# RWKV scan of a hybrid encoder step: head pairs on the column halves for the sample state, one y product for both chunks of a tile

## The reference, cut to what matters

```
def step(S, inp):                       # S: 64 x 64 per head, 8 heads
    r_t, w_t, k_t, v_t, kk_t, a_t = inp
    sa = einsum('bhij,bhj->bhi', S, -kk_t)
    S = S * w_t + sa (x) (kk_t * a_t) + v_t (x) k_t
    return S, einsum('bhij,bhj->bhi', S, r_t)      # y
S_fin, ys = lax.scan(step, S0, ...)
```

## Time and profile before

| what | value |
|---|---|
| median of 3 runs | 4723.28 us (4710.8 to 4728.6) |
| span of the profiled execution | 4722.2 us, 74875 instructions |
| median less the span | 1.1 us |
| PE busy | 4342.7 us, 92% of the span |
| DVE, ACT, POOL busy | 48%, 35%, 17% |
| mean granted TensorE clock | 0.971 of full speed |
| the eight sample state blocks (L1089 to L1091) | 5.72 us each |
| L1106, the y products of the chunks | x512 passes |

### The profile page before, as it was taken

The page is one execution under the profiler, slowest core; times in us unless marked ns, Lnnn a source line. Parts: engine busy times, 40 slices in busy tenths (PEclk is TensorE's granted clock), DMA queues, the critical chain, the costliest instruction groups (busy, mean ns, idle before and its releaser), DMA issues. The chain is left out here.

```text
span 4722.2 us, 74875 instructions
## 1 busy us (share of the span) xinstructions
PE 4342.7 (92%) x29488; PEld 3013.1 (64%) x29488; DVE 2275.1 (48%) x4684; ACT 1644.4 (35%) x3886; POOL 813.5 (17%) x980
## 2 busy tenths in 40 slices
PE   7999997989889989999979999979898899899999
PEld 3656665667666667777436666646676566677774
DVE  2555664345524463434425556643455344535344
ACT  4333333345533442212043333333555233421220
POOL 0011010000010015444300110000000100145443
PEclk8999998999999999999989999989999999999999
DMA  5110111110021112232241200120100211223222
GB/s 194 23 34 10 26 29 60 41 34 14 13 87 52 58 58 98 91 105 76 85 191 23 34 12 28 25 85 15 35 14 12 87 56 54 75 86 113 87 71 85
DMA packets 150654, 280.77 MB, mean 59 GB/s; under 512 B 51545, under 2 KB 77401, under 8 KB 145058
## 3 DMA queue, kind: packets, MB, share of 16 engines
q1 hardware_dynamic: 150306, 275.99, 18.3%
HBM read 230.96 MB, written 42.62 MB: 58 GB/s over the span
## 5 line engine op out<-in xcount | busy, mean ns | idle before, releaser
L1054 PE MATMUL banks<-hT,w_piece 128*128 128x384 f32 x1536 | 549.0, 499 | 8.4 <-ACT raw L1158 8.2
L1054 PEld LDWEIGHTS banks<-hT,w_piece 128*128 128x128 f32 x1536 | 281.4, 194 | 178.5 <-issue 15.1
L2232 PE MATMUL banks<-hT,w_piece 128*128 128x384 f32 x1056 | 354.1, 489 | 1.4 <-ACT sb_gate_raw L2342 1.4
L2232 PEld LDWEIGHTS banks<-hT,w_piece 128*128 128x128 f32 x1056 | 196.1, 190 | 141.4 <-issue 16.6
L1998 DVE SCALAR_TENSOR_TENSOR keysT<-banks,gains,rstd 64x128 f32<-64x128 f32 (+1 forms) x272 | 112.0, 412 | 248.1 <-ACT rstd L1912 245.5
L2688 DVE TENSOR_TENSOR gate_quarters<-gate_kept,banks 128x288 f32<-128x288 f32 x144 | 65.4, 454 | 299.0 <-PE banks L2551 294.0
L2639 ACT ACTIVATE gate_kept<-banks 128x288 f32<-128x288 f32 x144 | 59.1, 411 | 431.5 <-PE banks L2551 431.5
L2688 DVE TENSOR_TENSOR branch_quarters<-branch_kept,banks 128x288 f32<-128x288 f32 x144 | 65.4, 454 | 265.3 <-PE banks L2551 265.2
L2404 DVE TENSOR_TENSOR_SCAN left<-pass,zero 128x384 f32<-128x384 f32 (+7 forms) x144 | 189.8, 1318 | 5.0
L2401 DVE TENSOR_TENSOR pass<-pass,constants 128x128 f32<-128x128 f32 x128 | 41.5, 324 | 309.9 <-ACT take L2353 307.4
L1015 POOL TENSOR_TENSOR state_decayed<-state,decay_of_chunk 128x128 f32<-128x128 f32 x120 | 85.9, 716 | 578.7 <-DVE state L1287 578.7
(11 more groups left out here) (425 smaller groups left out, 9803.7 us busy)
## 6 DMA issues: line engine op xcount, KB each, us to landing
w_piece<-in_w_cols SPq DMA_DIRECT2D x66, 512.0 KB, 4.4
w_ada<-in_w_ada SPq DMA_DIRECT2D x24, 1024.0 KB, 10.5
w_gate_ahead<-in_w_cols SPq DMA_DIRECT2D x48, 512.0 KB, 4.3
w_branch<-in_w_br SPq DMA_DIRECT2D x96, 256.0 KB, 2.9
w_gate<-in_w_cols SPq DMA_DIRECT2D x48, 512.0 KB, 4.3
y_branch<-y_gated SPq DMA_DIRECT2D x12, 1152.0 KB, 8.4
sb_cached_keysT<-in_sbkT SPq DMA_DIRECT2D x8, 1024.0 KB, 7.6
sb_cached_values<-in_sbv SPq DMA_DIRECT2D x8, 1024.0 KB, 5.3
```

The lines of the kernel that those rows point to most:

```text
L1054: last = mm(dst, w[0 if kind in ("k", "v") else 1][:, k, :], hT[:, k, c], start=(k == 0), stop=(k == KD - 1))
L2232: last = mm(ps[:, bank[n], 0:TG], w_of[wn][:, k, :], hT[:, k, TG * g:TG * g + TG], start=(k == 0), stop=(k == KD - 1))
```

## The change: order of the sample products, and the y products

Three things are done. The sample products are issued head by head within each step rather than step by step within each head, in both places. The y products of even chunks are dropped, and those of odd chunks cover both chunks of the tile: 128 moving columns as two runs of 64 (`TM[:, i, 2:4, hc]`), two products per tile instead of four. For that both chunks' U write the same bank, `y_bank(i)`, in its columns 0 to 127 and 128 to 255; the second U has `start=False`. ACT and DVE follow the new places, and `y_ready` counts tiles instead of chunks.

```
+        def y_bank(i):
+            return 4 - 2 * (i % 2)
...
-            for hh in range(2):
-                hc = slice(64 * hh, 64 * hh + 64)
+            for hh, hc in enumerate(HALVES):
                 mm(ps[:, 4 + hh, :], R.WS[hc, :], S0[hc, :], start=True, stop=True)
+            for hh, hc in enumerate(HALVES):
                 last = mm(ps[:, 6 + hh, :], rows_of(RW[hc], i, 3), S0[hc, :], start=True, stop=True)
...
-            for hh in range(2):
-                hc = slice(64 * hh, 64 * hh + 64)
+            for hh, hc in enumerate(HALVES):
                 mm(ps[hc, 4, :], TM[:, i, 0, hc], wide[hh]..., start=True, stop=False, ...)
+            for hh, hc in enumerate(HALVES):
                 mm(ps[hc, 4, :], TM[:, i, 1, hc], wide[2 + hh]..., start=False, stop=False, ...)
+            for hh, hc in enumerate(HALVES):
                 last = mm(ps[hc, 4, :], ident[hc, hc], S0[hc, :], start=False, stop=True, ...)
...
-                ub = 4 + c - 2 * (i % 2)
-                if i >= 2:
+                yb = y_bank(i)
+                if c == 0 and i >= 2:
                     pe.wait_ge(y_copied, i - 1)
-                mm(ps[:, ub, 0:P], rows_of(RW, i, 4 - 2 * c), ST[:, :], start=True, stop=True).then_inc(u_ready, 1)
+                mm(ps[:, yb, P * c:P * c + P], rows_of(RW, i, 4 - 2 * c), ST[:, :], start=(c == 0), stop=True, ...).then_inc(u_ready, 1)
...
-                for hh in range(2):
-                    hc = slice(64 * hh, 64 * hh + 64)
-                    last = mm(ps[:, ub, hc], SI[:, i, hh, :], TM[:, i, 2 + c, hc], start=False, stop=True, ...)
-                last.then_inc(y_ready, 1)
+                if c == 1:
+                    both = ps[:, yb, 0:2 * P].rearrange("p (c n) -> p c n", c=2)
+                    for hh, hc in enumerate(HALVES):
+                        last = mm(both[:, :, hc], SI[:, i, hh, :], TM[:, i, 2:4, hc], start=False, stop=True, ...)
+                    last.then_inc(y_ready, 1)
```

More of the change, by code:

```diff
@@ L1096, in _ @@
                 pe.wait_ge(s_scaled, n + 2)
-                ub = 4 + c - 2 * (i % 2)
-                if i >= 2:
+                yb = y_bank(i)
+                if c == 0 and i >= 2:
                     pe.wait_ge(y_copied, i - 1)
-                mm(ps[:, ub, 0:P], rows_of(RW, i, 4 - 2 * c), ST[:, :], start=True, stop=True).then_inc(u_ready, 1)
+                mm(ps[:, yb, P * c:P * c + P], rows_of(RW, i, 4 - 2 * c), ST[:, :], start=(c == 0), stop=True, skip_group_check=True).then_inc(u_ready, 1)
                 fill(mid)
@@ L1103, in _ @@
                 mm(ps[:, 6, 0:P], TM[:, i, c, :], TM[:, i, 2 + c, :], start=True, stop=True).then_inc(s_ready, 1)
-                for hh in range(2):
-                    hc = slice(64 * hh, 64 * hh + 64)
-                    last = mm(ps[:, ub, hc], SI[:, i, hh, :], TM[:, i, 2 + c, hc], start=False, stop=True, skip_group_check=True)
-                last.then_inc(y_ready, 1)
+                if c == 1:
+                    both = ps[:, yb, 0:2 * P].rearrange("p (c n) -> p c n", c=2)
+                    for hh, hc in enumerate(HALVES):
+                        last = mm(both[:, :, hc], SI[:, i, hh, :], TM[:, i, 2:4, hc], start=False, stop=True, skip_group_check=True)
+                    last.then_inc(y_ready, 1)
                 fill(end)
@@ L1193, in _ @@
                     i = n // 2
[L1194 to L1197, removed]
+                    act.wait_ge(y_ready, i + 2)
+                    for c, rows in enumerate(HALVES):
+                        ins = ACTE.activation(Y[rows, i, :], ps[rows, y_bank(i), P * c:P * c + P], ACT.Copy)
+                    ins.then_inc(y_copied, 1)
                 if scan and n in (4, 8, 13, 16):
@@ L1280, in _ @@
                     dve.wait_ge(u_ready, n + 2)
-                    own(V.tensor_tensor(TM[uc, i, 2 + c, :], Z[uc, i, :], ps[uc, 4 + c - 2 * (i % 2), 0:P], ALU.add), u_added)
+                    own(V.tensor_tensor(TM[uc, i, 2 + c, :], Z[uc, i, :], ps[uc, y_bank(i), P * c:P * c + P], ALU.add), u_added)
                     dve.wait_ge(s_ready, n + 2)
```

## The result

The changed kernel takes 4684.85 us (median of 4 runs, 4681.44 to 4694.05) against 4718.57 us before (4 runs): ratio 0.9927, interval 0.9907 to 0.9946. The medians differ by 33.7 us, and the interval of the ratio stands for 25 to 44 us. The prediction said 4691 us, with a range of 4678 to 4705, so it held.

The account below looks back on a forecast made before the run. PE, busy 92% of the span, was taken to bound the kernel, with savings counting in full only where it doesn't wait. 22.8 + 0 + 9.2 = 32 us off 4722.2 gave span 4690, median 4691 us, range 4678 to 4705.

Parts of the forecast that it names:

- The sample state block: Block before each scan's chunk loop: both heads take one head's 2.86 us instead of 5.72, saving 22.8 us in eight scans.
- column halves don't pair: Rival on the sample state block: no overlap there, only 9.2 us left, 4714 us; chance 0.05.
- The first products: Samples' first products in each scan: row halves already run side by side at 1.79 us, so saving 0.
- so they stood in the code: Sample state block: reason given for 12 passes on two column halves running strictly one after another before.
- The rival's price for this term: Samples' first products: four of eight passes unpaired before, so 1.79 becomes 0.9, 7 us in eight scans, 4684; chance 0.06.
- The y products: Chunk loops: four passes dropped per even chunk, saving 6.4 us in six prep scans and 2.8 in two gate scans.
- Each even chunk brings the next U forward by 0.39, each odd one sets it back by 0.05: Prep scan loops: per-chunk price in us of the changed y products, before losses to waits.
- the same chunk table: Prep scan loop: chunk-by-chunk count of y savings kept or lost to waits, about 1.1 us per scan.
- whole 0.39: Gate scan loops: the full even-chunk saving in us, kept where S(3) waits for DVE and DVE for ACT.
- slower: the clock: Rival in prep loops: longer chunk 1 wait lowers PE's clock, costing 6.8 us a scan, 4732 if all six; chance 0.05.
- The sum: Whole kernel: 22.8 + 0 + 9.2 = 32 us off the profiled 4722.2, median 4691 us, 0.68% faster.

Follow-up runs that it names:

- e_col: Kernel before with only the sample state block reordered, heads alternating within each step; ratio 0.9949 to the kernel before.
- e_row: Kernel before with only the samples' first four products reordered, both heads with WS, then both with the r rows; ratio 0.9999.
- e_near: Kernel before with the state block's two 128-row products issued head by head, both heads' identity products last; 4705.73 us in one run.
- e_far: Kernel before with the state block's 128-row products head by head, each head's second one issued twice, identity products last; 4701.73 us in one run.
- e_early1: Changed kernel with two end fills of chunk 1 moved ahead of S in prep scans; ratio 0.9909 to the kernel before.
- e_pad: Changed kernel with two unread 64-column dummy products put back behind S in each even chunk; ratio 0.9952 to the kernel before.
- e_y: Kernel before with only the y products changed: none in even chunks, 128 columns in odd ones; ratio 0.9961.
- after: The changed kernel with all three parts, against the kernel before: 4684.85 us, ratio 0.9927; its profiled span is 4679.6 us.
- e_early: Changed kernel with two end fills each of chunks 1 and 8 moved ahead of S in prep scans; ratio 0.9919 to the kernel before.
- e_wide: Kernel before with each y product 128 moving columns wide instead of 64, still two per chunk; 4729.72 us in one run.

## Why the prediction was right, step by step

**The sample state block, 22.8 us.** Right: 5.72 became 2.87 in the prep scans and the gate scans gained 2.83 each, 22.7 by the parts, 24 by e_col. Adjacent products on the two column halves start 7 to 14 ns apart, with 512 columns as with L1868's 128. The rival "column halves don't pair" is out.

**The first products, 0.** Right: 1.79 us before and after, and e_row can't be told from the kernel before. The rule of the Trainium skill ("TensorE: Matmul & The Clock Gate", section "Step-by-step: what each phase is for") that matmuls keep program order would have given a gain here; this trace doesn't agree. In the earlier trace rows, e_near and e_far passes for a free half of the array run before passes that stand ahead of them. The same behaviour explains why one reordering was worth nothing; with the limit that C0 sets it also fits that the other halved the block. The prediction took the block's missing overlap from the earlier trace rows and gave as its reason "so they stood in the code". That alone can't be the reason: the first products stood apart in the code too and paired, and e_near shows that one product between the heads would have done no harm in the block either. So the two terms came out right by the rows, not by an account that covers both. The rival's price for this term was wrong as well: 1.79 us is what four pairs at 0.45 take, so all eight passes were paired already, and no reordering could have brought 0.9.

**The y products, 9.2 us.** The mechanism was right and the size too small: 8.5 in the six prep scans (1.42 each) and 2.9 in the two gate scans, 11.4. The 2.9 come from two profiles that both had chunk 9 at a low clock in both gate scans, so they compare like with like. The step that failed is the price: "Each even chunk brings the next U forward by 0.39, each odd one sets it back by 0.05". Measured are 0.45 and 0.00 in the prep scans. The forward steps come in the chunks that the prediction named: against before, S(n) of the first prep scan is early by 0, 0, 0, 0.45, 0.44, 0.89, 0.89, 0.89, 0.88, 1.33, 1.32, 1.32, 1.33, 1.45, 1.41, 1.41 us for n = 0 to 15. Kept in chunks 2, 4 and 8, lost in 0, 6, 10 (foretold 0.06) and 14, 0.13 in 12 (foretold 0.08). With the right price the same chunk table gives 3 x 0.45 + 0.13 = 1.48 less the 0.04 lost between S(13) and S(14), which is 1.44 where 1.42 was measured. S(1) came no earlier and waited 1.61 (foretold 1.55): there chunk 0's saving went, and e_early1 took 1.29 out of this wait.

In the gate scans an even chunk is 0.20 shorter, as foretold (0.44 in chunk 10), and chunks 3 and 7 are another 0.24 shorter, which is the "whole 0.39" at the new price; chunks 1, 5 and 9 are 0.10 longer and chunk 13 is 0.21 longer, which the prediction did not have. The loops of e_pad and e_y differ by the y products alone, and chunk 9 ran at the full clock in both. First e_pad, then e_y, windows of the second gate scan's loop, columns as in rows 2:

```profile
3072.12:3120.25 48.13, 36.44 (x189) 24.34 (x188) 24.10 (x71) 20.10 (x34) 6.09 (x15) 0.99 0.06 22
```

```profile
3082.44:3128.95 46.51, 34.46 (x156) 20.29 (x155) 24.11 (x71) 20.10 (x34) 6.09 (x15) 0.99 0.06 22
```

That is 1.6 us in this scan, where 1.4 was foretold.

**Waits and clock in the loop.** The rival "slower: the clock" was wrong in its place: the window of the prep loop shows 1.00. It was right that the clock at a scan's start is worth several us, but there it changed in both directions. In the first gate scan chunk 9 took 3.95 us at 0.57 in `after` and 2.35 at 1.00 in e_y, with the same code. The kernel before had the low clock there too, so it is no cost of the change in this comparison. First `after`, then e_y, windows from U to U of chunk 9, columns as in rows 2:

```profile
741.01:744.96 3.95, 3.95 (x12) 2.91 (x13) 0.84 (x3) 1.04 (x5) 0.80 (x2) 0.57 0.00 0
```

```profile
757.31:759.66 2.35, 2.35 (x13) 1.67 (x14) 0.84 (x3) 0.68 (x4) 0.58 (x2) 1.00 0.00 0
```

**The sum.** Foretold 32; block and loops give 22.7 + 11.4 = 34.1; the runs say 33.7 and, again, 28 (4721.6 x 0.006). So the hit in the total rests on two terms that were right and a third that was 2.2 too small. The 16.9 us at the starts that the two profiles show are not a gain of the change that can be claimed: the kernel before had them at 5.0 in another execution. Nor is the 8.4 in the rest a cost: both are granted clock, and they happened to offset each other in part. Starts and rest together lie between 3997 and 4021 in all thirteen profiles, 4001 and 4012 for the changed kernel, 4009 and 4004 for the one before.

**Open.** What lowers the clock at a scan's start. Kernels with prep loops of 69.85 had some long starts in all profiles but e_far's, those with 68.44 one or none, and e_early and e_early1, whose loops are shorter still, had three and four again. So neither the y products nor a shorter loop decides it alone, and e_pad's first start differs from that of `after` with the same code ahead of it. Each kernel was profiled once or twice, which is too little to tell a habit from chance; that it depends on how the lengths of the earlier stages line up is only a guess. Open is also what exactly stops the overlap at C0.

## What to carry to other kernels

Put products that use different halves of the array next to each other; but look in the trace first whether they already overlap, as those did here that had one other product of the same shape between them. Price a removed product by what the next ones lose as well, not by the distance to the next start: a pass of 64 columns cost as much as one of 128, so joining two narrow products with the same weights saved one of them for nothing. Then follow the saving chunk by chunk to the next wait; where it ends in one, move work that doesn't depend on it into that wait, which brought 1.29 us a loop here. And before you compare two profiles of the same stage, compare the granted clock in them.

## What the runs showed of the hardware

- Four float32 passes of 64 moving columns and four of 128, each with its weight load, both take 0.772 us up to the second fill pass behind them (before, e_wide); single passes of 128 follow each other at 0.11 us, passes of 384 at 0.322. Two runs of 64 columns in one product cost the same as one of 128 (0.44 for four passes, `after` and e_wide).
- Two passes on different column halves start 7 to 14 ns apart and together take as long as one: eight passes of 512 columns in 1.86 us (233.44 to 235.30), where four took 1.86 before.
- A pass for a free half of the array ran ahead of three passes that stand before it in the program (e_near, e_far, the first products), and not over more in these blocks. It did not run over, or beside, a product of another shape (the block of before, the end of e_far's block); whether the shape is the reason is not shown.
- The same 54 passes took 15.79 us at a granted clock of 1.00 and 21.80 at 0.69, in programs with the same code there (`after`, e_pad). Over everything outside the scans, two executions of the changed kernel differed by 10.7 us with the clock (4000.9 and 4011.6).
